# A two-block network on one core: the second experts' ring begun in the output projection, step sizes made with heads on partitions, eight slots for the first experts, and matmuls that fill waits

## The chip, the cores and the metric

The kernel runs on one core of one Trainium2 chip. The metric is the device time of the whole program in microseconds (us), the median of several runs; lower is better. TensorE is called PE, VectorE DVE, ScalarE ACT, GpSimd POOL and SyncE SP, as in the profile.

## The reference

The input x is 512 tokens of width 1024, and all data is float32. Two blocks follow one another.

The first block projects the tokens (and 256 context tokens) into neighbourhood attention and a bidirectional state-space scan with 32 heads in each direction. For the scan, each token has a step size per head and direction, `dt = softplus(dt_raw + bias)`, where `dt_raw` is 64 columns of the input projection; with `a = -dt * exp(a_log)` the scan needs sums of `a` over the tokens of each piece of 128 (four pieces of x, two of the context): up to each token, after it, and over the whole piece. The 24 tiles of the scan's inputs pass a convolution over five tokens. Branches, gates and an output projection close the mixer. Then come 16 experts, each of which takes the 64 tokens that rate it highest:

```python
gate, idx = lax.top_k(jnp.transpose(aff, (0, 2, 1)), cap)
hid = silu(xg @ w_eg) * (xg @ w_eu)
yo = (hid @ w_ed) * gate
```

The second block has an RWKV mixer, latent attention and an output projection `w_out`, and then 32 smaller experts, of which each token uses two; a last rmsnorm with a gain gives the output.

## The kernel before, in words

The program is a row of stages. Each stage is a block in which every engine runs its own list in order and waits on semaphores; the next block begins when all engines have left the last one. Float32 matmuls appear in the trace as two PE instructions each, transposes as one. Weights come over SP's DMA queue, mostly in pieces of 2 MB (`PIECE`, 16 KB on each of 128 partitions).

**The convolution stage**, `steps_and_conv`. PE first makes the step-size products: for each of six pieces of tokens and each of eight blocks of the contraction it loads 128 tokens as weights and streams 64 columns of `w_dt` (L1119), 48 matmuls in all. DVE adds the bias; then come an exponential and a logarithm on ACT and a chain of small DVE operations (L1240 to L1252) which ends in `a`. Meanwhile PE begins the 24 tiles (L1141): 8 matmuls of 512 columns each, and from the fifth tile on also 8 of 256 columns for the context (L1147). Each tile needs one of two banks, and a bank comes free when DVE has convolved its tile (`main_taken`). DVE's order is: bias and signs, tile 0, the chain, tile 1, tile 2 and so on. After tile 3, PE makes the sums: 36 matmuls of 32 columns (L1130), whose exponentials ACT makes. From tile 5 on PE turns the finished tiles back.

**The first experts.** `route_tokens` norms the rows, scores them, and turns the affinities so that experts lie on partitions (L2255, waits for `aff_ready`). DVE then finds the 64 best of each (L2288 to L2294) in eight rounds of two operations, PE waits for `chosen_T`, turns the marks back (L2259) and counts them (L2265). `stream_experts` gathers tokens with matmuls (L2040) and streams 192 weight pieces through a ring of `EC_SLOTS` = 7 slots. The first 7 are loaded in `route_tokens`; SP loads piece n once PE is done with piece n - 7. The eight pieces of the first pair's gate weights are the first eight.

**The end of the second mixer.** `project_rows_onto` multiplies by `w_out` in two halves of 512 columns (stage `p_out2`), each loaded in the stages before. Its input `u2T` was freed after it.

**The second experts.** `RoundsRing` has nine slots of one piece. `route_experts` loads the router's weights and the constants, then pieces 0 to 2, then waits for the normed rows, stores them to memory (`hm_xn_rows`), and loads pieces 3 to 8. `fine_experts` builds the token lists of each pair of experts (L3657), gathers the rows by an indirect DMA from POOL (L3637), turns them (`flips`, L3665), and multiplies (`hidden`, L3677, and `down`, L3696). POOL also issues for each first piece an indirect DMA which would load other experts in a second round and moves nothing in the first (`load_again`, L1905); `hidden` waits for it too. SP reloads a slot when its product is done, 39 pieces in all.

**The last norm**, `final_norm`. ACT squares and sums four tiles of rows, then takes one root of all four; DVE takes the reciprocal and scales the four tiles, each of which SP stores.

Of the kernel before, what the change touches and what calls it, by code (L numbers as in the profile page):

```python
# [15 lines left out]
P = 128  # L16
D = 1024
# [262 lines left out]
def rows_view(x):  # L280

    return x[0].rearrange("(t p) d -> p t d", p=P)

# [789 lines left out]
def steps_and_conv(k, hT, hcT, steps_in, weights, vec, taps, work, dt, a, dec, bcT, b_rows, bc_rows, xs, xsc):  # L1073
# [9 lines left out]
    with ctx:  # L1083
        main, side = ps("main", [P, 2, 512]), ps("side", [P, 2, 512])
        flip, flip_c = ps("flip", [P, 2, 512]), ps("flip_c", [P, 2, 512])
        prod, sums = flip[:, 0, :], (flip[:, 1, :], flip_c[:, 0, :], flip_c[:, 1, :])
# [86 lines left out]
        def _(act):  # L1173
# [14 lines left out]

            act.wait_ge(steps_loaded, 16 * 5)
# [6 lines left out]
            for i in range(3):  # L1196
                act.activation(dec[:, 4 * i:4 * i + 4, :].rearrange("p m n -> p (m n)"), sums[i][:, 0:384], ACT.Exp).then_inc(exp_out, 1)
# [413 lines left out]
def project_rows_onto(k, label, w, kt, xT, residual, n_chunks, ahead):  # L1611
# [13 lines left out]
    project(k, label, w, kt, 512, n_chunks, groups, add, ahead=ahead, first=wait_loaded)  # L1625
# [190 lines left out]
EC_SLOTS = 7  # L1816
# [43 lines left out]
HM_SLOTS = 9  # L1860

# [9 lines left out]
class RoundsRing:  # L1871
# [3 lines left out]
    def __init__(self, k, scope):  # L1875
# [8 lines left out]
        self.tile = scope.enter_context(k.nc.sbuf_tensor("hm_ring", [P, HM_SLOTS, PIECE], F32))  # L1884
        self.rows = scope.enter_context(k.nc.sbuf_tensor("hm_again_rows", [P, 2 * LT], mybir.dt.uint32))
        self.first_loaded = [k.semaphore(f"hm_first_loaded{n}") for n in range(HM_SLOTS)]
        scope.callback(lambda: k.clear(self.first_loaded))

    def load_first(self, sp, slots):
        for n in slots:  # L1890
            sp.dma_start(*second_weights(self.k, self.tile[:, n, :], *self.order[n])).then_inc(self.first_loaded[n], 16)
# [4 lines left out]
    def load_again(self, pool, n):  # L1896
        kind, u, e = self.order[n]
        pool.wait_ge(self.first_loaded[n], 16)
        if kind == "gu":
            parts = [(self.tile[:, n, :], self.k.dram["moe_w_gu_2"][0].rearrange("e (p a) n -> (e p) (a n)", p=P), 2 * u + e)]  # L1900
        else:
            parts = [(self.tile[:, n, i * PIECE // 2:(i + 1) * PIECE // 2], self.k.dram["moe_w_down_2"][0].rearrange("e (p f) n -> (e p) (f n)", p=P), 2 * u + i)
# [9 lines left out]
    def load(self, sp, n):  # L1912
        sp.dma_start(*second_weights(self.k, self.tile[:, n % HM_SLOTS, :], *self.order[n])).then_inc(self.loaded[n % HM_SLOTS], 16)

    def wait(self, pe, *job):
# [6 lines left out]
        return self.tile[:, n % HM_SLOTS, :]  # L1922
# [273 lines left out]
def route_tokens(k, norm, out, router, columns, ring, rank, aff):  # L2196
# [8 lines left out]
    with ctx:  # L2205
# [35 lines left out]
        def _(pe):  # L2241
# [1089 lines left out]
def second_mixer(k, x_in, dump=None):  # L3331
# [16 lines left out]
    with ExitStack() as outer:  # L3348
        uT = tile(outer, "u2T", [P, KD, L])
        with ExitStack() as mid:  # L3350
# [552 lines left out]
```

## Time and profile before

| | |
|---|---|
| median of 3 runs | 3594.27 us (3591.18 to 3597.16) |
| the profiled execution | 3598.31 us, of which the span 3596.5 us |
| busy: PE, weight loads, DVE, ACT, POOL | 3148.0, 1667.6, 1070.2, 558.9, 286.4 us |
| moved by DMA | 669.33 MB, mean 186 GB/s |
| mean granted clock of PE | 0.931 of full speed |

The span runs from the first to the last instruction of the profiled execution. Matmuls are pipelined, so a group's time includes a modelled end. The granted clock of PE is 1.00 (2.4 GHz) or 0.50 (1.2 GHz); a number between says that a stretch has both. GB/s and the DMA share (1.00: all 16 engines busy) show where the weights set the pace.

### The profile page before, as it was taken

To read this page: it belongs to the slowest core of one execution; us is meant where nothing else is said; L and a number is where in the kernel's file an instruction comes from. 1 tells how busy PE (TensorE), PEld (TensorE's weight loads), DVE (VectorE), ACT (ScalarE), POOL (GpSimd) and SP (SyncE) were. 2 spreads that over 40 slices of the span, in tenths; PEclk is the share of its full clock that TensorE was granted. 3 is DMA by queue.
4 is the path that set the end of the run, shared out by engine and by line. 5 is a ranking of instruction groups with operands and counts; after the bars stand their busy time and mean duration, and the time that the engine had idled before them with its cause. 6 is when DMAs were issued, how large, how long until landed. Compare 5 with 4: busy or idle time off the path is not lost. (4 is left out here: it accounts for less than half of the span.)

```text
span 3596.5 us, 37828 instructions
## 1 busy us (share of the span) xinstructions
PE 3148.0 (88%) x15792; PEld 1667.6 (46%) x15792; DVE 1070.2 (30%) x2063; ACT 558.9 (16%) x1178; POOL 286.4 (8%) x270
## 2 busy tenths in 40 slices
PE   6997889998899999698999999987996789995984
PEld 5444645664554444453344434433545763643331
DVE  2233702454573301410111011103056553522112
ACT  2002510112452200100000000002022221301111
POOL 0003000002761000000000000000002200001000
PEclk9998998998899999699999999998998999996997
DMA  7721021110001222379999999996310021017996
GB/s 264 257 71 47 2 74 35 47 36 0 24 1 47 94 70 70 164 295 428 424 425 428 424 424 412 421 423 277 128 35 2 3 109 49 12 59 275 404 425 259
DMA packets 132079, 669.33 MB, mean 186 GB/s; under 512 B 17578, under 2 KB 45645, under 8 KB 98889
## 3 DMA queue, kind: packets, MB, share of 16 engines
q1 hardware_dynamic: 115385, 630.24, 43.5%
q10 hardware_dynamic: 11488, 28.31, 2.1%
q0 software_dynamic: 5040, 8.40, 0.7%
q8 instruction: 124, 2.03, 0.2%
q14 instruction: 42, 0.34, 0.0%
HBM read 672.15 MB, written 14.69 MB: 191 GB/s over the span
## 5 line engine op out<-in xcount | busy, mean ns | idle before, releaser
L1992 PE MATMUL ec_wide<-ec_ring,ec_xg 128*64 128x512 f32 x2048 | 456.7, 600 | 20.8 <-issue 15.4
L1992 PEld LDWEIGHTS ec_wide<-ec_ring,ec_xg 128*64 128x64 f32 x2048 | 148.1, 138 | 309.3 <-issue 305.1
L2026 PE MATMUL ec_acc<-ec_ring,ec_hidT 128*64 128x512 f32 x1024 | 238.8, 622 | 36.4 <-DMA ec_ring<-in_w_exp_down 34.5
L2151 DVE TENSOR_SCALAR ec_xg<-ec_piece,ordered 128x128 f32<-128x128 f32 x64 | 21.9, 405 | 579.7 <-PE ec_piece L2040 579.7
L2026 PEld LDWEIGHTS ec_acc<-ec_ring,ec_hidT 128*64 128x64 f32 x1024 | 84.9, 143 | 188.1 <-issue 188.1
L3677 PE MATMUL hm_gu<-hm_ring,hm_xg 128*64 128x512 f32 x512 | 121.3, 629 | 15.8 <-DMA hm_ring<-in_moe_w_gu,hm_again_rows 7.7
L2040 PEld LDWEIGHTS ec_piece<-ec_sel,x 128*128 128x128 f32 x512 | 122.9, 336 | 8.6 <-issue 5.7
L2040 PE MATMUL ec_piece<-ec_sel,x 128*128 128x128 f32 x512 | 124.4, 406 | 2.8 <-DVE ec_sel L2133 2.8
L2727 POOL TENSOR_TENSOR solve_T<-const_rw,solve_T 128x512 f32<-128x512 f32 x8 | 10.1, 1266 | 1321.3 <-DVE solve_T L2765 1321.3
L2115 ACT ACTIVATE ec_hidT<-ec_acc 128x512 f32<-128x512 f32 x32 | 17.4, 594 | 516.1 <-PE ec_acc L2015 516.1
L1141 PE MATMUL conv_main<-hT,conv_early 128*128 128x512 f32 x192 | 86.2, 605 | 1.6 <-DVE bcT L1217 1.6
L561 PE MATMUL p_rkv_acc<-ahead_rkv,h2mT 128*128 128x384 f32 x256 | 85.9, 500 | 1.9 <-DVEq L569 1.9
L1141 PE MATMUL conv_main<-hT,conv_late 128*128 128x512 f32 x192 | 86.8, 607 | 0.0
L3677 PEld LDWEIGHTS hm_gu<-hm_ring,hm_xg 128*64 128x64 f32 x512 | 39.8, 145 | 94.4 <-issue 92.7
L1389 ACT ACTIVATE ssd_seg_in<-const_all,a 128x128 f32<-128x128 f32 x256 | 77.8, 389 | 0.5 <-PEq L1083 0.5
L2166 DVE TENSOR_TENSOR branch<-branch,ec_piece 128x512 f32<-128x512 f32 x64 | 44.0, 688 | 108.8 <-PE ec_piece L2058 108.8
L1349 PE MATMUL ssd_seg<-ssd_seg_in,const_all 128*128 128x512 f32 x128 | 62.8, 614 | 10.0 <-DVE ssd_cbm L1411 10.0
L2058 PE MATMUL ec_piece<-ec_y,ec_selT 128*128 128x512 f32 x128 | 63.8, 623 | 7.3 <-DVE ec_selT L2160 6.1
L561 PEld LDWEIGHTS p_rkv_acc<-ahead_rkv,h2mT 128*128 128x128 f32 x256 | 50.2, 196 | 37.4 <-issue 2.7
L3696 PE MATMUL hm_acc<-hm_ring,hm_hidT 128*64 128x512 f32 x256 | 64.3, 649 | 2.1 <-ACT hm_hidT L3728 1.6
L2772 DVE TENSOR_TENSOR solve_T<-solve_T,solve_wide 64x512 f32<-64x512 f32 (+1 forms) x80 | 50.6, 632 | 50.0 <-PE solve_wide L2658 42.0
L1375 PE MATMUL ssd_yd<-ssd_xd,ssd_lx 128*128 128x64 f32 x512 | 61.6, 274 | 2.1 <-DVE ssd_lx L1415 2.1
(624 smaller groups left out, 4957.3 us busy)
## 6 DMA issues: line engine op xcount, KB each, us to landing
ec_ring<-in_w_exp_gate SPq DMA_DIRECT2D x64, 2048.0 KB, 13.6
ec_ring<-in_w_exp_up SPq DMA_DIRECT2D x64, 2048.0 KB, 22.2
ec_ring<-in_w_exp_down SPq DMA_DIRECT2D x64, 2048.0 KB, 17.3
hm_ring<-in_moe_w_gu SPq DMA_DIRECT2D x32, 2048.0 KB, 27.3
hm_ring<-in_moe_w_down SPq DMA_DIRECT2D x16, 2048.0 KB, 29.1
ahead_qkv<-in_w_in SPq DMA_DIRECT2D x10, 2048.0 KB, 9.6
key<-in_w_ada ACTq DMA_DIRECT2D x4, 2048.0 KB, 8.7
v<-in_w_ada ACTq DMA_DIRECT2D x4, 2048.0 KB, 10.2
```

What stands on the lines that cost most here:

```text
L561: last = pe.matmul(acc[0:rows, bank, 0:cols], stat(j), mov(j), start=(j == 0), stop=(j == kt - 1))
L1141: last = pe.matmul(main[:, i % 2, :], w[:, j, m * P:(m + 1) * P], hT[:, j, :], start=(j == 0), stop=(j == KD - 1))
L1349: pe.matmul(seg[:, h, :], k.const("after" if d == 0 else "before"), seg_in[:, m % 2, 4 * h:4 * h + 4].rearrange("p h l -> p (h l)"), start ...
L1375: last = pe.matmul(yd[:, m % 2, h * 64:(h + 1) * 64], lx[:, m % 2, h, :], xd[:, n % 2, h * 64:(h + 1) * 64], start=True, stop=True)
L1389: ins = act.activation(seg_in[:, m % 2, h, :], cum, ACT.Copy, scale=a[:, tile(units[mains[m]]), col:col + 1])
L1992: last = pe.matmul(wide[half(e), b, :], xg[:, u % 2, j, half(e)], w[e][:, a, b * 512:(b + 1) * 512], start=(j == 0), stop=(j == KD - 1))
L2026: last = pe.matmul(acc[half(e), h, :], hidT[:, f, half(e)], w[e][:, r, h * 512:(h + 1) * 512], start=(f == 0), stop=(f == FT - 1))
L2040: last = pe.matmul(piece[:, m % 2, i * P:(i + 1) * P], x[:, t, HALF * h + i::KD], sel[:, t, :], start=(t == 0), stop=(t == LT - 1))
L2058: pe.matmul(piece[:, m % 2, :], selT[:, t * P:(t + 1) * P], y[:, h * 512:(h + 1) * 512], start=True, stop=True).then_inc(piece_done, 1)
L2772: dve.tensor_tensor(x, x, wide[s][half(c), c, first * 256:512], ALU.subtract).then_inc(T_done[s], 1)
L3677: last = pe.matmul(gu[half(e), u % 2, :], xg[:, u % 2, j, half(e)], w[e][:, j, :], start=(j == 0), stop=(j == KD - 1))
L3696: last = pe.matmul(acc[half(e), h, :], hidT[:, u % 2, f * P + e * SLOTS:f * P + (e + 1) * SLOTS], view[:, e * FT + f, h * 512:(h + 1) * 51 ...
```

## The change

1. `steps_and_conv`: the products are made with `w_dt` as weights (64 columns, so that heads lie on partitions) and the tokens streaming, 8 matmuls of 512 columns and 8 of 256. ACT copies them to SBUF, and after tile 0 PE turns them with six transposes (`step_rows`). The sums are 6 matmuls of 192 columns in place of 36 of 32.
2. `EC_SLOTS` is 8.
3. `keep_clocked` issues matmuls whose result nobody reads: 12 before the wait for `aff_ready`, 72 before that for `chosen_T`, and 12 in `fine_experts` ahead of the first turn.
4. `u2T` stays allocated through the second experts and becomes the last of the nine slots. Seven slots are placed before `p_out2`, and their loads are issued there by SP (`also`); the last two are loaded in `route_experts`. SP's six loads behind the store of the rows are gone.
5. `final_norm` loads the root's table first, and takes root, reciprocal and scaling tile by tile.

The rest of the diff is indentation in `second_mixer`.

```diff
+def keep_clocked(k, pe, bank, n):
+    for _ in range(n):
+        pe.matmul(bank[:, 0:P], k.const("ones"), k.const("ident"), start=True, stop=True)
...
-        prod, sums = flip[:, 0, :], (flip[:, 1, :], flip_c[:, 0, :], flip_c[:, 1, :])
+        prod, sums = flip[:, 1, :], (flip[:, 0, :], flip_c[:, 0, :], flip_c[:, 1, :])
+        stepsT = work[0:64, 3, 2 * n:2 * n + L + CTX]
...
                 pe.wait_ge(steps_loaded, 16 * 5)
+                for bank, src, width in ((flip, hT, L), (flip_c, hcT, CTX)):
+                    for j in range(KD):
+                        last = pe.matmul(bank[0:64, 0, 0:width], w_dt[:, j, :], src[:, j, :], start=(j == 0), stop=(j == KD - 1))
+                    last.then_inc(products_T, 1)
+
+            def step_rows():
+                pe.wait_ge(steps_taken, 2)
                 for t in range(N_SEG):
-                    src, c = (hT, t) if t < LT else (hcT, t - LT)
-                    for j in range(KD):
-                        last = pe.matmul(prod[:, t * 64:(t + 1) * 64], src[:, j, c * P:(c + 1) * P], w_dt[:, j, :],
-                                         start=(j == 0), stop=(j == KD - 1))
+                    last = pe.transpose(prod[:, t * 64:(t + 1) * 64], stepsT[:, t * P:(t + 1) * P], k.const("ident", 64)[:, 0:64])
                 last.then_inc(product_ready, 1)
...
-                for d in range(2):
-                    for t in range(N_SEG):
-                        m = d * N_SEG + t
-                        for i, name in enumerate((("upto", "after", "ones"), ("from", "before", "ones"))[d]):
-                            c = (m % 4) * 96 + i * 32
-                            last = pe.matmul(sums[m // 4][:, c:c + 32], k.const(name), a[:, t, d * 32:(d + 1) * 32], start=True, stop=True)
+                for i, names in enumerate((("upto", "from"), ("after", "before"), ("ones", "ones"))):
+                    for d, name in enumerate(names):
+                        last = pe.matmul(sums[i][:, d * N_SEG * 32:(d + 1) * N_SEG * 32].rearrange("p (t h) -> p t h", h=32), k.const(name),
+                                         a[:, :, d * 32:(d + 1) * 32], start=True, stop=True)
...
                 project_tile(i)
+                if i == 0:
+                    step_rows()
...
+            act.wait_ge(products_T, 1)
+            act.activation(stepsT[:, 0:L], flip[0:64, 0, :], ACT.Copy).then_inc(steps_taken, 1)
+            act.wait_ge(products_T, 2)
+            act.activation(stepsT[:, L:L + CTX], flip_c[0:64, 0, 0:CTX], ACT.Copy).then_inc(steps_taken, 1)
...
-EC_SLOTS = 7
+EC_SLOTS = 8
...
             norm.turn(pe, scores)
+            keep_clocked(k, pe, norm.pt[:, 0, :], 12)
             pe.wait_ge(aff_ready, 1)
...
             last.then_inc(wide_ready, 1)
+            keep_clocked(k, pe, norm.pt[:, 0, :], 72)
             pe.wait_ge(chosen_T, 1)
...
-            project_rows_onto(k, "p_out2", k.dram["w_out_2"][0], KD, uT, k.residual, 2, ahead)
+    k.rounds_ring = RoundsRing(k, k.second_scope, uT[:, :, :].rearrange("p j n -> p (j n)"))
+    project_rows_onto(k, "p_out2", k.dram["w_out_2"][0], KD, uT, k.residual, 2, ahead,
+                      also=lambda sp: k.rounds_ring.load_first(sp, range(HM_HEAD)))
...
-            ring.load_first(sp, range(3))
+            ring.load_first(sp, range(HM_HEAD, HM_SLOTS))
             sp.wait_ge(norm.row_ready, LT)
             sp.dma_start(xn_rows.rearrange("(t p) d -> p t d", p=P), norm.xn[:, :, :]).then_inc(xn_stored, 16)
-            ring.load_first(sp, range(3, HM_SLOTS))
...
             lists(1)
+            pe.wait_ge(index_ready, 2)
+            keep_clocked(k, pe, list_, 12)
             flips(0)
...
+            act.preload_act_table(ACT.Sqrt)
             for t in range(LT):
                 link(act.activation(square[:, :], x[:, t, :], ACT.Square, accum_out=ss[:, t:t + 1]))
-            act.activation(rstd[:, :], ss[:, :], ACT.Sqrt, scale=1.0 / D, bias=k.const("eps")).then_inc(root_ready, 1)
+                act.activation(rstd[:, t:t + 1], ss[:, t:t + 1], ACT.Sqrt, scale=1.0 / D, bias=k.const("eps")).then_inc(root_ready, 1)
...
-            link(dve.reciprocal(rstd[:, :], rstd[:, :]))
             for t in range(LT):
+                dve.wait_ge(root_ready, t + 1)
+                link(dve.reciprocal(rstd[:, t:t + 1], rstd[:, t:t + 1]))
```

## Rows read from the trace of the kernel before

**Rows 1.** Stretches (us from the start): busy time and count of each engine, PE clock, DMA share, GB/s

```profile
582.00:603.00 21.00, 20.55 (x97) 20.58 (x98) 0.09 (x1) 1.54 (x2) 0.00 (x0) 0.52 0.32 100
```

**Rows 2.** Timeline of PE in the convolution stage: start, length, instruction, count, wait before

```profile
582.45 13.59 PE L1119 MATMUL conv_flip<-w_dt,hT 128*128 128x64 f32 x64 [2.60 <-PEq L1058]
...
602.66 22.82 PE L1141 MATMUL conv_main<-hT,conv_early 128*128 128x512 f32 x48
627.12 7.13 PE L1141 MATMUL conv_main<-hT,conv_early 128*128 128x512 f32 x16 [1.64 <-DVE bcT L1217]
634.09 2.76 PE L1130 MATMUL conv_flip<-a,const_all 128*128 128x32 f32 x24
636.68 9.80 PE L1130 MATMUL conv_flip_c<-a,const_all 128*128 128x32 f32 x48
646.30 9.46 PE L1141 MATMUL conv_main<-hT,conv_late 128*128 128x512 f32 x16
655.60 3.62 PE L1147 MATMUL conv_side<-hcT,conv_late 128*128 128x256 f32 x16
```

**Rows 3.** Timeline of DVE in the same stage: tile 0, the chain's first operation, tile 1

```profile
611.78 0.75 DVE L1213 TENSOR_SCALAR bcT<-conv_main,taps 128x512 f32<-128x512 f32 x1 [7.33 <-PE conv_main L1141]
...
615.59 0.35 DVE L1240 TENSOR_SCALAR y<-y 128x384 f32<-128x384 f32 x1
...
623.18 0.74 DVE L1213 TENSOR_SCALAR bcT<-conv_main,taps 128x512 f32<-128x512 f32 x1
```

**Rows 4.** Timeline of PE in the first routing and at the first gather

```profile
1506.05 1.02 PE L2255 MATMUL route_wide<-const_all,ec_aff 128*16 128x128 f32 x4 [1.59 <-DVE ec_aff L2286]
1520.49 0.61 PE L2259 MATMUL route_score<-const_all,route_chosenT 16*128 16x16 f32 x4 [13.42 <-DVE route_chosenT L2294]
1521.42 4.45 PE L2265 MATMUL route_spread<-route_chosen,const_all 128*128 128x16 f32 x20 [0.32 <-DVE route_chosen L2296]
1528.65 15.55 PE L2040 MATMUL ec_piece<-ec_sel,x 128*128 128x128 f32 x64 [2.79 <-DVE ec_sel L2133]
```

**Rows 5.** A stretch in that gather: columns as in rows 1

```profile
1534.50:1536.00 1.50, 1.50 (x9) 1.50 (x7) 0.00 (x0) 0.00 (x0) 0.00 (x0) 0.80 0.00 0
```

**Rows 6.** Stretches of the first experts: all of the stream, and a slow one

```profile
1556.00:2474.00 918.00, 856.45 (x3720) 370.90 (x3716) 110.81 (x264) 43.63 (x71) 0.00 (x0) 0.98 1.00 423
2200.00:2250.00 50.00, 50.00 (x220) 17.42 (x222) 10.04 (x20) 2.17 (x4) 0.00 (x0) 1.00 0.99 409
```

**Rows 7.** Waits of PE in the first experts: us in total, times, longest

```profile
PE ec_acc L2026 <- DMA ec_ring<-in_w_exp_down: 34.5, 18, 2.7
```

**Rows 8.** A stretch that holds most of the output projection

```profile
3198.00:3246.00 48.00, 48.00 (x113) 21.32 (x112) 4.82 (x7) 0.00 (x0) 0.00 (x0) 1.00 0.00 0
```

**Rows 9.** Timeline at the start of the second experts: gather, empty load, turn, product

```profile
3289.04 1.20 POOL L3637 DMA_INDIRECT hm_xrow<-hm_xn_rows,hm_index  x1 [0.91 <-POOL hm_xrow L3631]
...
3293.54 0.99 POOL L1905 DMA_INDIRECT hm_ring<-in_moe_w_gu,hm_again_rows  x1 [0.31 <-issue]
...
3298.85 1.97 PE L3665 MATMUL hm_flip<-const_all,hm_xrow 128*128 128x128 f32 x8 [8.90 <-DMA hm_xrow<-hm_xn_rows,hm_index]
...
3308.56 9.49 PE L3677 MATMUL hm_gu<-hm_ring,hm_xg 128*64 128x512 f32 x32 [7.74 <-DMA hm_ring<-in_moe_w_gu,hm_again_rows]
```

**Rows 10.** The eleven empty loads of L1905, from issue to landing

```profile
DMA to landing us min/median/max: 4.7/10.0/14.9
```

**Rows 11.** Timeline of PE: one later pair's first product

```profile
3353.81 7.04 PE L3677 MATMUL hm_gu<-hm_ring,hm_xg 128*64 128x512 f32 x32
```

**Rows 12.** A stretch of the second experts' stream: columns as in rows 1

```profile
3350.00:3540.00 190.00, 170.42 (x814) 71.10 (x814) 30.11 (x58) 22.49 (x37) 11.86 (x12) 0.94 1.01 425
```

**Rows 13.** Timeline of the last norm, ACT and DVE

```profile
3580.61 1.06 ACT L3813 ACTIVATE final_square<-x 128x1024 f32<-128x1024 f32 x1 [23.03 <-PEq L3854]
...
3585.32 1.28 ACT L3814 ACT_TABLE_LOAD   x1
...
3587.16 4.87 DVE L3823 SCALAR_TENSOR_TENSOR final_y<-x,final_rstd,final_gain 128x1024 f32<-128x1024 f32 x4
```

More of the change, by code:

```diff
@@ L1196, in _ @@
             for i in range(3):
-                act.activation(dec[:, 4 * i:4 * i + 4, :].rearrange("p m n -> p (m n)"), sums[i][:, 0:384], ACT.Exp).then_inc(exp_out, 1)
+                act.activation(dec[:, :, 32 * i:32 * i + 32], sums[i][:, 0:2 * N_SEG * 32].rearrange("p (m h) -> p m h", h=32), ACT.Exp).then_inc(exp_out, 1)
             act.wait_ge(exp_out, 6)
@@ L1608, in branch, with project_rows_onto @@
     project(k, label + "_b", w, feats, width, D // width, groups, merge, link_steps=1 if add else 0, ahead=ahead, then=then)
-def project_rows_onto(k, label, w, kt, xT, residual, n_chunks, ahead):
+def project_rows_onto(k, label, w, kt, xT, residual, n_chunks, ahead, also=None):
     x = residual.tile
@@ L1623, in wait_loaded @@
         dve.wait_ge(residual.loaded, 16)
-    project(k, label, w, kt, 512, n_chunks, groups, add, ahead=ahead, first=wait_loaded)
+    project(k, label, w, kt, 512, n_chunks, groups, add, ahead=ahead, first=wait_loaded, also=also)
 def project_rows(k, label, w, kt, xT, out, n_chunks, width=512, ahead=None, then=None, also=None):
@@ L1860 @@
 HM_SLOTS = 9
+HM_HEAD = HM_SLOTS - 2
 def second_weights(k, place, kind, u, e):
@@ L1871, with __init__ @@
 class RoundsRing:
-    def __init__(self, k, scope):
+    def __init__(self, k, scope, last):
         self.k = k
@@ L1883, in __init__, with complete @@
         self.index = {job: n for n, job in enumerate(self.order)}
-        self.tile = scope.enter_context(k.nc.sbuf_tensor("hm_ring", [P, HM_SLOTS, PIECE], F32))
-        self.rows = scope.enter_context(k.nc.sbuf_tensor("hm_again_rows", [P, 2 * LT], mybir.dt.uint32))
+        self.head = scope.enter_context(k.nc.sbuf_tensor("hm_ring", [P, HM_HEAD, PIECE], F32))
+        self.places = [self.head[:, n, :] for n in range(HM_HEAD)] + [None, last]
         self.first_loaded = [k.semaphore(f"hm_first_loaded{n}") for n in range(HM_SLOTS)]
         scope.callback(lambda: k.clear(self.first_loaded))
+    def complete(self, scope):
+        self.places[HM_HEAD] = scope.enter_context(self.k.nc.sbuf_tensor("hm_ring_late", [P, PIECE], F32))[:, :]
+        self.rows = scope.enter_context(self.k.nc.sbuf_tensor("hm_again_rows", [P, 2 * LT], mybir.dt.uint32))
     def load_first(self, sp, slots):
         for n in slots:
-            sp.dma_start(*second_weights(self.k, self.tile[:, n, :], *self.order[n])).then_inc(self.first_loaded[n], 16)
+            sp.dma_start(*second_weights(self.k, self.places[n], *self.order[n])).then_inc(self.first_loaded[n], 16)
     def enter(self, sem):
@@ L1912, in load @@
     def load(self, sp, n):
-        sp.dma_start(*second_weights(self.k, self.tile[:, n % HM_SLOTS, :], *self.order[n])).then_inc(self.loaded[n % HM_SLOTS], 16)
+        sp.dma_start(*second_weights(self.k, self.places[n % HM_SLOTS], *self.order[n])).then_inc(self.loaded[n % HM_SLOTS], 16)
     def wait(self, pe, *job):
@@ L1921, in wait @@
             pe.wait_ge(self.loaded[n % HM_SLOTS], 16 * (n // HM_SLOTS))
-        return self.tile[:, n % HM_SLOTS, :]
+        return self.places[n % HM_SLOTS]
 def stream_experts(k, ring, x, rstd, rank, gate, scale_cols, shift_cols, out):
@@ L3606, in fine_experts @@
         BACK = 2 * LT
-        back = ring.tile[:, 0:BACK * D // PIECE, :].rearrange("p s (b n) -> p (s b) n", n=D)
+        back = ring.head[:, 0:BACK * D // PIECE, :].rearrange("p s (b n) -> p (s b) n", n=D)
         gu, turn, acc, flip, list_ = ps("gu", [P, 2, 512]), ps("turn", [P, 512]), ps("acc", [P, 2, 512]), ps("flip", [P, 2, 512]), ps("list", [P, 512])
@@ L3836, in second_experts @@
         out = k.residual.tile
-        with ExitStack() as s:
-            ring = RoundsRing(k, s)
+        with k.second_scope as s:
+            ring = k.rounds_ring
+            ring.complete(s)
             ordered = tile(s, "hm_ordered", [P, KD])
@@ L3873, in two_blocks @@
         k.ordered = tile(everything, "ordered", [P, 2, KD])
-        k.branch_scope = ExitStack()
+        k.branch_scope, k.second_scope = ExitStack(), ExitStack()
         first_mixer(k, dram["x"])
```

187 lines of the change are left out of this document (93 added, 94 removed).

## The prediction, made before the changed kernel was run

> **What bounds the kernel now.** No single resource does: each stage has its own. I read first the stretches of the whole span, then in each stage that the change touches the timeline of PE, then that of the engine or queue that PE waits for.
>
> In the convolution stage PE is the bound. From 582.45 to 655.60, from the step products to the end of tile 4's 512-column matmuls, it stands still only for the 1.64 us ahead of tile 3 [rows 2]. But its clock is at 0.52 while it makes the step products [rows 1], which are 96 small instructions, and the 48 later sums (9.80 us) take 0.204 us each where the first 24 (2.76 us) took 0.115 [rows 2]: both clock levels in one list. The tiles that follow pay too: 9.46 us where a tile takes 7.03 to 7.13 [rows 2].
>
> In the first experts DMA is the bound: from 1556 to 2474 all 16 engines are busy (share 1.00, 423 GB/s), and PE waits for weights 18 times, 34.5 us in all [rows 6, 7]. The stream begins when PE gives back the first slot, soon after the first gather [rows 4].
>
> At the start of the second experts the ring's own first filling is in the way. The gather issued at 3289.04 is turned at 3298.85 and `hidden(0)` begins at 3308.56, after waits of 8.90 and 7.74 us for DMA [rows 9]; no product waits there. After that DMA is again the bound (share 1.01, 425 GB/s) [rows 12], so what the first product gains, the end gains. The last norm is a plain chain [rows 13].
>
> **Step products and sums.** Old, to the end of tile 4's main matmuls: 655.60 - 582.45 = 73.15 us [rows 2]. New: 16 instructions of 512 columns at the 7.03 us of a tile and 16 of 256 at 3.62 us [rows 2], about 10.5 without the modelled ends. The old products ran at half clock, and the three tiles behind them lost 22.82 - 3 x 6.9 = 2.1 us till the clock was back; I charge the same 2.1 at the entry (0 if the clock holds). Tile 0: 6.9. Then DVE leads. In the old kernel tile 3 starts 627.12 - 611.7 = 15.4 us after tile 0 is ready: its convolution (611.78 to 615.59), the chain (to 623.18), tile 1 (to 627.1) [rows 2, 3]. In the new one the bias and signs no longer hide behind tile 0, because they follow `step_rows`. Six transposes and their latency are about 0.9 us (four turns take 0.61 or 1.02 at half clock [rows 4]), three DVE operations of 384 columns, between 0.35 and 0.75 each [rows 3], about 1.5. So tile 3 starts 17.8 us after tile 0, and PE waits some 3.4 us ahead of it. Tile 3: 6.9. Sums: 12 instructions of 192 columns at 6.9/16 x 192/512 = 0.16 us, 1.9 with 0.2 of latency. Tile 4: 6.9. I add 1 us for a clock that may fall in the 3.4 us wait. Sum: 10.5 + 2.1 + 6.9 + 17.8 + 6.9 + 2.1 + 6.9 + 1.0 = 54.2. **Saved: 19 us**, between 15 (the clock falls at both places and the tiles after wait too) and 22 (it never falls). ACT's two copies hide behind tile 0; if they didn't, only `step_rows` would move. The exponentials of the sums are the same three and stand ahead of tile 5's end. The convolution weights are asked for by PE's progress with an idle queue (share 0.32 even in the busiest part [rows 1]).
>
> **Eighth slot.** A piece takes 918/185 = 4.96 us of the stream [rows 6]. Eight pieces lie ready instead of seven, 184 are left, the start is the same event. PE can follow: its 34.5 us of waits [rows 7] is slack that it uses up first. **Saved: 5 us**; 3 if part of the waits isn't given back, 5 at most. The eighth load has room before the stream begins: the queues are empty during the gather (share 0.00) [rows 5].
>
> **The 84 filling matmuls of the first routing.** PE works in order, so what they overrun delays the chain to the first gather, and with it the whole stream. A call is two instructions with 128 weight columns. The nearest rows are the sums: 0.115 us at full clock, 0.204 at half [rows 2], so 0.22 or 0.41 a call (a shade less without the latency). The 12 take 2.6 to 4.9 us in a wait of 1.59 us; the 72 take 15.5 to 29.4 us in a wait of 13.42 us [rows 4]. The clock is at half when they start; the gather, also of 128 columns, brought it back some 6 us after its start [rows 4, 5]. I take that: the 12 at half clock, 3.3 us late, and nearly all 72 at full, 2.6 us more than their wait, so PE turns the marks back about 6 us later than now. Given back: 4.45 us of counts become 2.3, and 0.61 becomes 0.4, so 2.4 us. The gather itself gains nothing: its 64 instructions take 0.243 us each on both sides of the change of clock [rows 4, 5]. **Lost: 3.5 us**, between 0 (full clock at once) and 9 (it comes late).
>
> **The ring begun in the output projection.** Seven pieces are 35 us of DMA. In 3198 to 3246 the queues carry nothing (share 0.00) [rows 8], so they are down by about 3230, ahead of the router's small loads. SP has nothing else to issue there; `w_out`'s second half is ahead of them in the same queue. The last two pieces and the store of the rows are 15 us of DMA early in the routing, and the store has two pieces ahead of it, not three, and none behind. So at 3289 DMA is idle. The gather should land in about 4.7 us, the shortest that the empty loads took [rows 10], at 3293.8. The 12 filling calls wait for the second list, about 1.1 us after the gather's issue (an estimate: POOL issues the second gather and the first empty load before 3293.54 [rows 9]), and run from 3290.2 to 3295.1 at half clock; the turn takes 1.97 [rows 9] and DVE's scaling of 1024 elements 1.2 to 1.3 (4.87/4 [rows 13]), together 3298.4. The second empty load, issued at 3293.54, lands at 3298.2 [rows 9, 10]. `hidden(0)` starts at about 3298.4 instead of 3308.56. **Saved: 10 us**, 7 if the empty load is slow by itself (its median is 10.0 [rows 10]), 11 if an idle queue is faster than any row. The stream behind it is DMA-bound [rows 12] and moves with it.
>
> Its first product takes 9.49 us where later ones take 7.04 [rows 9, 11], and the clock shapes the second too; the 12 calls may bring it back before. Between 0 and 5 us; I take **2 us**. Here a row and a rule differ in what they promise: what lies between the calls and the product is eight transposes and DVE's scaling.
>
> **Last norm.** Old: 3580.61 to 3592.03, 11.4 us [rows 13]. New: table 1.28, first squares and root 1.5, then four times DVE's 0.2 + 1.25, 8.8 us. The gain's load starts with the stage and may hold the first row; **saved 2 us**, between 1 and 3.
>
> **Sum.** 19 + 5 - 3.5 + 10 + 2 + 2 = 34.5 us. The profiled execution took 3598.3, so 3563.8 on its scale; it stands 4.0 us above the median of the runs. On the median: 3594.3 - 34.5 = 3559.8.
>
> **Rivals.** (a) *The clock stays at half through the filling matmuls of the routing.* For it: the 20 instructions of the counts, back to back, still ran at half clock (4.45 us) [rows 4]. Against: the gather of the same width brought it back [rows 5]. Then 72 calls take 29.4 us, PE is 3.3 + 16 us late and the counts gain nothing: 19.3 lost in place of 3.5, 3575.6. Chance 0.09.
> (b) *The clock is half again at `hidden(0)`.* The turn in the old kernel takes 1.97 us, half clock's time [rows 9]. Then the 2 us go: 3561.8. Chance 0.22. The Trainium skill's page "TensorE: Matmul & The Clock Gate" ("Part 4: PE-mode transpose") says that transposes don't count as busy for the clock; by that rule the eight turns give up what the twelve calls won, and the time is this rival's. No row of ours has such a burst followed by turns alone.
> (c) *PE, not DMA, paces the first experts once the slot is there,* and the eighth gives 0: 3564.8. PE was busy 856 of 918 us [rows 6]. Against it stand 18 waits up to the end [rows 7]. Chance 0.06.
> (d) *The ring's seven loads hold up `w_out`'s second half.* If all eight transfers shared the queue, it would land 40 us after the stage's start, and PE wants it in the middle of a stage of some 55 us, of which 48 are in [rows 8]: about 11 us late, 3570.8. Chance 0.04.
> (e) *Slower than before:* one more transfer in flight lowers the rate of the first experts' stream. The stretch at 2200 had 409 GB/s with the engines no less busy [rows 6]. 184 pieces take 913 us at 423 GB/s; each 1% of rate is 9 us, and from 3.8% (407 GB/s, all through) the kernel is slower than before; at 5% about 3606. Against: the queue is full already and its depth alone would be new. Chance 0.02.
> (f) *The reordered start of the convolution costs more than its 2.4 us,* say tile 1's convolution held by ACT's tables: half the 19 us gone, 3569. Chance 0.06.
>
> **Chances and range.** My forecast has the remaining 0.51. From the terms' bounds it alone reaches from 3551 to 3569; (b) and (c) lie inside. Taking in (d), (f) and most of (a), and some luck with the clock below, the range is 3548 to 3574. About 0.2% (7 us) is what a measurement here tells from no change. Only (e), or several bounds together, reach 3587: faster 0.96, within 0.2% 0.01, slower 0.03.
>
> **What would show it.** Right: tile 3's first matmul 36 to 39 us after the products' first (44.7 now [rows 2]), with a wait of 3 to 4 us ahead; twelve sums in about 2 us; a stream of 184 pieces at 423 GB/s; L2259 some 5 to 7 us later after the scores than now; no DMA between 3230 and the router's loads (on the old scale); `hidden(0)` 9 to 11 us sooner after the gather's issue; 9 us of last norm. Wrong: the 72 calls in over 20 us; a wait of PE for `w_out`; a new DMA wait for the empty loads; a stream rate under 415 GB/s.

## The result, and the profile after

The changed kernel takes 3548.98 us (median of 4 runs, 3546.7 to 3553.64) where the kernel before, on the same chip, takes 3593.66 (3591.18 to 3597.16): a ratio of 0.9877, 95% interval 0.986 to 0.9894, 44.7 us saved. On two more chips the ratio was 0.9871 and 0.9876. The prediction was 34.5 us saved, 3559.8 us; the result lies at the low end of its range (3548 to 3574), and below the 3551 to 3569 that the forecast's own terms reached. The profiled executions have spans of 3596.5 and 3548.5 us, so 48.0 us are to be found between them. The same events in both, in us from the start:

| event | before | after | difference | since the row above |
|---|---|---|---|---|
| first step product | 582.45 | 582.60 | +0.15 | |
| behind tile 4's wide matmuls | 655.60 | 636.69 | -18.91 | -19.06 |
| first routing: first turn of PE | 1480.48 | 1459.76 | -20.72 | -1.81 |
| first gather on PE | 1528.65 | 1510.74 | -17.91 | +2.81 |
| last weights of the first experts used | 2484.3 | 2453.3 | -31.0 | -13.1 |
| second experts: first gather issued | 3289.04 | 3259.00 | -30.04 | +1.0 |
| `hidden(0)` begins | 3308.56 | 3267.76 | -40.80 | -10.76 |
| its weights given back (SP reloads) | 3318.08 | 3274.89 | -43.19 | -2.39 |
| last product read out | 3556.56 | 3510.52 | -46.04 | -2.85 |
| last norm begins | 3580.61 | 3535.50 | -45.11 | +0.93 |
| its last multiplication ends | 3592.03 | 3544.64 | -47.39 | -2.28 |

The timeline of PE in the convolution stage of the changed kernel (start, length, instruction, count, the wait before it and what ended it), to be read beside [rows 2]:

```profile
582.60 8.75 PE L1126 MATMUL conv_flip<-hT,w_dt 128*64 128x512 f32 x16 [2.60 <-PEq L1064]
591.18 3.62 PE L1126 MATMUL conv_flip_c<-hcT,w_dt 128*64 128x256 f32 x16
594.73 7.13 PE L1151 MATMUL conv_main<-hT,conv_early 128*128 128x512 f32 x16
601.79 0.58 PE L1132 MATMUL conv_flip<-const_all,y 64*128 64x64 f32 x6
602.31 14.00 PE L1151 MATMUL conv_main<-hT,conv_early 128*128 128x512 f32 x32
619.21 8.83 PE L1151 MATMUL conv_main<-hT,conv_early 128*128 128x512 f32 x16 [2.90 <-DVE bcT L1233]
627.88 0.81 PE L1139 MATMUL conv_flip<-a,const_all 128*128 128x192 f32 x4
628.53 1.46 PE L1139 MATMUL conv_flip_c<-a,const_all 128*128 128x192 f32 x8
629.83 7.03 PE L1151 MATMUL conv_main<-hT,conv_late 128*128 128x512 f32 x16
```

The 96 narrow products have become 12 us. The sums, 72 instructions in 12.2 us before, are now 12 in 1.95 us. Both falls of the clock are to be seen: 8.75 us where a tile takes 7.03 to 7.13, and 8.83 behind the wait of 2.90 us.

The same view in the first routing and at the first gather, beside [rows 4]:

```profile
1483.57 4.79 PE L288 MATMUL route_pt<-const_all 128*128 128x128 f32 x24
...
1488.64 16.24 PE L288 MATMUL route_pt<-const_all 128*128 128x128 f32 x144
...
1505.55 2.40 PE L2288 MATMUL route_spread<-route_chosen,const_all 128*128 128x16 f32 x20 [0.32 <-DVE route_chosen L2319]
1510.74 15.55 PE L2061 MATMUL ec_piece<-ec_sel,x 128*128 128x128 f32 x64 [2.79 <-DVE ec_sel L2154]
```

Twelve calls at half clock in 4.79 us, 72 at full clock in 16.24, no wait behind either; the counts take 2.40 in place of 4.45, and the gather the same 15.55 as before.

Stretches of the whole stream of the first experts (length, busy time of the engines, then the clock of PE, the DMA share and GB/s), and PE's waits in it, beside [rows 6, 7]:

```profile
1538.00:2445.00 907.00, 854.14 (x3718) 368.12 (x3716) 110.69 (x264) 43.63 (x71) 0.00 (x0) 0.98 1.00 426
```

```profile
PE ec_acc L2047 <- DMA ec_ring<-in_w_exp_down: 28.4, 14, 2.7
```

The rate is 426 GB/s where it was 423. Less than 1%, but of 900 us.

The timeline at the start of the second experts, beside [rows 9]:

```profile
3259.00 1.20 POOL L3660 DMA_INDIRECT hm_xrow<-hm_xn_rows,hm_index  x1 [0.90 <-POOL hm_xrow L3654]
...
3259.69 5.49 PE L288 MATMUL hm_list<-const_all 128*128 128x128 f32 x24 [0.25 <-DVE hm_index L3775]
...
3264.97 1.48 PE L3688 MATMUL hm_flip<-const_all,hm_xrow 128*128 128x128 f32 x8
...
3266.48 1.22 DVE L3781 TENSOR_TENSOR hm_xg<-hm_flip,hm_ordered 128x1024 f32<-128x1024 f32 x1 [6.17 <-PE hm_flip L3688]
...
3267.76 7.09 PE L3700 MATMUL hm_gu<-hm_ring,hm_xg 128*64 128x512 f32 x32 [1.32 <-DVE hm_xg L3781]
```

Neither the turn nor the product waits for DMA any longer; the DMA share in 3258 to 3275 is 0.16. The eleven empty loads now land in (beside [rows 10]):

```profile
DMA to landing us min/median/max: 2.1/2.9/9.7
```

And the last norm, beside [rows 13]:

```profile
3535.52 0.34 SPq L3828 DMA_DIRECT2D final_gain<-in_final_norm_g  x1
3536.79 1.06 ACT L3839 ACTIVATE final_square<-x 128x1024 f32<-128x1024 f32 x1
...
3537.97 0.29 ACT L3840 ACTIVATE final_rstd<-final_ss,const_all 128x1 f32<-128x1 f32 x1
...
3538.98 0.16 DVE L3848 RECIPROCAL final_rstd<-final_rstd 128x1 f32<-128x1 f32 x1 [5.89 <-DMA final_gain<-in_final_norm_g]
...
3543.36 1.28 DVE L3849 SCALAR_TENSOR_TENSOR final_y<-x,final_rstd,final_gain 128x1024 f32<-128x1024 f32 x1
```

The gain's load, 3.44 us from issue to landing on the chain that ended last, is what DVE waits for; the first root is ready at 3538.26, 0.7 us sooner.

So most terms came out as forecast, and one did not: between the first gather and the last weights of the first experts the changed kernel gained 13.1 us where one piece of 4.96 us was charged.

### The profile page after: what moved, and what is told of

It reads as the page before. It is cut to its first block and busy times, and to the rows that moved or that the text cites. A ratio compares the mean times of both kernels' runs of the same rounds, so it can differ in the third digit from the quotient of the medians.

```text
span 3548.5 us, 38000 instructions
## 1 busy us (share of the span) xinstructions
PE 3138.4 (88%) x15866; PEld 1657.4 (47%) x15866; DVE 1070.3 (30%) x2066; ACT 560.3 (16%) x1183; POOL 287.7 (8%) x270
## 5 line engine op out<-in xcount | busy, mean ns | idle before, releaser
L2047 PE MATMUL ec_acc<-ec_ring,ec_hidT 128*64 128x512 f32 x1024 | 233.6, 611 | 29.2 <-DMA ec_ring<-in_w_exp_down 28.4
L1391 PEld LDWEIGHTS ssd_yd<-ssd_xd,ssd_lx 128*128 128x128 f32 x512 | 61.2, 196 | 2.9 <-DVE ssd_lx L1431 2.9
## 6 DMA issues: line engine op xcount, KB each, us to landing
ec_ring<-in_w_exp_gate SPq DMA_DIRECT2D x64, 2048.0 KB, 17.7
```

The lines of the kernel that those rows point to most:

```text
L1391: last = pe.matmul(yd[:, m % 2, h * 64:(h + 1) * 64], lx[:, m % 2, h, :], xd[:, n % 2, h * 64:(h + 1) * 64], start=True, stop=True)
L2047: last = pe.matmul(acc[half(e), h, :], hidT[:, f, half(e)], w[e][:, r, h * 512:(h + 1) * 512], start=(f == 0), stop=(f == FT - 1))
```

## Experiments

### The eighth slot

```
EC_SLOTS = 8   again: unchanged
EC_SLOTS = 7   slots7
EC_SLOTS = 6   slots6
EC_SLOTS = 8   before8, in the kernel before (there it was 7)
```

Expected of the changed kernel run once more:

> The changed kernel once more. The stream of the first experts ran at 426 GB/s in its first profile (1538 to 2445) and at 423 in the kernel before (1556 to 2474). Theory A (the rate belongs to the eighth slot): 426 to 428 GB/s again, and 43 to 48 us saved. Theory B (the rate is drawn anew in each execution): it may come out at 420 to 424 this time, and then the span is 6 to 9 us longer than 3548.5. The clock's phase alone may move the span by 2 to 3 us.

Expected with seven slots:

> The changed kernel with seven slots in the first experts' ring; nothing else. Forecast (one reload fewer, one piece of 4.96 us): 5 us slower than the changed kernel, stream at the same rate. Theory A (eight transfers under way also keep the rate up): 12 to 14 us slower, stream at 422 to 424 GB/s with stretches under 420. Theory B (rate drawn anew): 5 us by the medians, whatever the rate in the profile. Rival C (PE paces the stream): no difference.

Expected of the kernel before with eight:

> The kernel before with eight slots in the first experts' ring; nothing else. Forecast: 5 us faster than the kernel before, all of it between the first gather and the last weights. Theory A: 12 to 14 us faster, stream at 426 to 428 GB/s. Theory B: 5 us by the medians. Rival C: no difference.

Expected with six, after these three were known:

> The changed kernel with six slots in the first experts' ring; nothing else. Eight slots went to seven at a price of 17 us. Theory A (with fewer slots the queue runs dry at the places of each pair of experts where PE gives nothing back for up to 21.7 us): the dry spells grow faster than the slots shrink, 30 to 70 us slower than with seven, with 10 us stretches under 300 GB/s. Rival D (a full queue moves more bytes a second than a less full one, everywhere): some 17 us again, and a rate that is lower in all stretches. Forecast of the prediction (one reload for each slot): 5 us.

The column "stream" is from the first product of the first experts to the last use of their weights in the profile. "Missing" sums what the rate lacks of 428 GB/s, as time, over stretches of 10 us from 12 to 14 us after the stream's start to near its end (what is above 428 is taken off).

| kernel | slots | median, us | ratio to the kernel before | stream, us | missing, us |
|---|---|---|---|---|---|
| before | 7 | 3596.59 | 1 | 938.6 | 10.2 |
| before8 | 8 | 3580.05 | 0.995 (0.9936 to 0.9964) | 925.5 | 2.1 |
| again | 8 | 3551.73 | 0.9871 (0.9856 to 0.9886) | 926.0 | 3.1 |
| slots7 | 7 | 3569.01 | 0.9919 (0.9905 to 0.9932) | 950.7 | 22.0 |
| slots6 | 6 | 3598.28 | 1.0012 (1.0002 to 1.0021) | 977.4 | 44.3 |

The first four medians are of one chip: the slot is worth 16.5 us in the kernel before and 17.3 us in the changed one. That is nearest to theory A, and more than its 12 to 14 us. Theory B falls: the eleven profiles with eight slots (those of the runs below among them) have streams of 923.8 to 928.5 us, and the two with seven 938.6 and 950.7. The two with seven slots are one profile each of two kernels, and that of slots7 was the slowest of its five executions (3573.26 us); why they differ by 12 us wasn't tried. So the 13.1 us between the first two profiles are one draw, and the medians' 17 the better figure. Rival C falls too. slots6 ran on another chip, beside a fourth run of the changed kernel (again2, below): 48.2 us slower than that, so the second slot is worth some 31 us, the low end of what theory A gave (30 to 70). The two columns on the right say how a longer stream divides, not why: with seven slots the stream is 24.7 us longer than in again, of which one reload is 4.96 and the missing time 22.0 - 3.1 = 18.9; with six it is 51.4 longer, two reloads and 41.2 us.

Where the time is missing is seen in stretches of 10 us. First the kernel with six slots, then the one with seven, then the changed kernel, each around 1700:

```profile
1690.00:1700.00 10.00, 10.00 (x44) 10.00 (x43) 1.37 (x4) 0.00 (x0) 0.00 (x0) 1.00 0.99 421
1700.00:1710.00 10.00, 10.00 (x46) 6.06 (x47) 3.24 (x12) 0.00 (x0) 0.00 (x0) 1.00 0.71 301
1710.00:1720.00 10.00, 9.13 (x42) 3.07 (x40) 1.38 (x2) 0.00 (x0) 0.00 (x0) 1.00 0.79 316
...
1750.00:1760.00 10.00, 10.00 (x52) 3.83 (x52) 0.00 (x0) 1.09 (x2) 0.00 (x0) 1.00 1.02 436
```

```profile
1690.00:1700.00 10.00, 10.00 (x45) 7.38 (x46) 3.27 (x13) 0.00 (x0) 0.00 (x0) 1.00 1.02 431
1700.00:1710.00 10.00, 9.13 (x42) 3.07 (x40) 1.38 (x2) 0.00 (x0) 0.00 (x0) 1.00 0.96 393
1710.00:1720.00 10.00, 10.00 (x36) 3.20 (x34) 3.44 (x5) 0.00 (x0) 0.00 (x0) 1.00 0.94 356
```

```profile
1700.00:1710.00 10.00, 9.12 (x40) 3.11 (x39) 1.38 (x2) 0.00 (x0) 0.00 (x0) 1.00 1.00 428
1710.00:1720.00 10.00, 10.00 (x38) 3.21 (x38) 4.50 (x7) 0.00 (x0) 0.00 (x0) 1.00 1.00 428
```

The engines of DMA are idle for up to three tenths of these stretches (share 0.71), while PE is busy for over nine tenths of them; outside these places the rate with six slots is as high as with eight (436; 26 of its 95 stretches are at 430 or more, and 28 of the 90 of again), so rival D, which wanted it lower everywhere, falls. The place comes back every 120 us, once for each pair of experts. What happens there shows in the timelines of PE and of SP's issues with six slots:

```profile
1688.63 15.55 PE L2061 MATMUL ec_piece<-ec_sel,x 128*128 128x128 f32 x64
1704.12 7.09 PE L2013 MATMUL ec_wide<-ec_ring,ec_xg 128*64 128x512 f32 x32
```

```profile
1668.95 20.59 SPq L1852 DMA_DIRECT2D ec_ring<-in_w_exp_up  x6
1711.24 10.38 SPq L1852 DMA_DIRECT2D ec_ring<-in_w_exp_gate  x4
```

PE makes the gather of the next pair, 15.5 us of small matmuls that use no weights of the ring, and then a product of 7.1 us before it gives any back. SP issues nothing from 1689.5 to 1711.2: its longest wait is 21.7 us in the kernels with six, seven and eight slots alike. The ring must hold enough that is asked for and not yet landed to carry the queue over this.

How much that is can be counted from the traces: the pieces that SP has issued, less the bytes of its queue that have landed. In the six later pairs some 4.5 pieces land between the two issues. The wait begins with 3.6 to 4.2 pieces on their way with six slots, with 4.3 to 5.2 with seven (in slots7 and in the kernel before) and with 5.4 to 6.2 with eight. It ends with none, with 0 to 0.6 and with 0.9 to 1.7. So six slots run dry, seven all but dry, and eight keep about a piece or more.

The kernel before had the same holes, flatter. Its gather ends at 2190.3 and SP's next issue is at 2197.5; the rate is lowest after that:

```profile
2208.00:2218.00 10.00, 10.00 (x39) 3.18 (x39) 4.82 (x7) 0.00 (x0) 0.00 (x0) 1.00 0.96 385
2218.00:2228.00 10.00, 10.00 (x44) 3.15 (x39) 4.54 (x12) 0.00 (x0) 0.00 (x0) 1.00 0.96 377
```

The same two stretches have 429 GB/s in before8. Idle engines are only part of what is missing: 377 is 0.88 of 428, and the share is 0.96. Summed over all stretches, the lower share makes up about 34 of the 41.2 us with six slots, and about 10 of the 18.9 with seven. The rest passed with the engines counted as busy, behind the places where few pieces were on their way. Why they move less then wasn't tried; rival D may hold there, though not everywhere.

### The filling calls of the first routing

```
-            keep_clocked(k, pe, norm.pt[:, 0, :], 12)     no84: gone    trim, best: 4
-            keep_clocked(k, pe, norm.pt[:, 0, :], 72)     no84: gone    trim: 50    best: 58
```

> The changed kernel without the 84 filling calls of the first routing (12 and 72); they compute nothing that is used. My step: the calls overrun the waits by some 5 us and give back 2.3 us in marks and counts, so without them the time from the end of the scores to the first gather is 2.8 us shorter (27.1 in the changed kernel, about 24.3 here) and the kernel 3 us faster; marks take 0.61 and counts 4.45 us again. Rival (the calls' clock reaches the gather and the first pieces): the gather takes longer than 15.55 us or the first pieces run at half clock for longer, and the kernel is 0 to 5 us slower than the changed one.

> The changed kernel with 4 and 50 filling calls in the first routing in place of 12 and 72; they compute nothing that is used. If the calls only cost what they overrun the waits by, and keep the clock: the marks are turned back some 15.5 to 16.5 us after the end of the scores (21.2 in the changed kernel, 16.0 without calls in the kernel before), in 0.4 us, the counts take 2.4, and the kernel is 4.5 to 5.5 us faster than the changed one and 2 us faster than the one without calls. Rival (the clock comes back too late in fewer calls): the counts take 4.45, and 50 calls run past their wait; 0 to 3 us faster.

Measured: without calls 3549.63 us, 2.1 less than the changed kernel on the same chip (ratio 0.987, 0.9855 to 0.9885), which the times alone can't tell from nothing. The trace can: from the first turn to the first gather it is 48.1 us (1458.7 to 1506.84), where the changed kernel takes 50.9 to 51.0 and the kernel before 48.2. The calls cost 2.8 us, as stepped; the gather is no slower for their absence, so the rival falls.

With 4 and 50 calls: 3544.15 us, ratio 0.985 (0.9834 to 0.9867), 4 to 6 us less than the changed kernel by the times, as expected. But that agreement is luck: from turn to gather it takes 47.9 us, 3.1 less than the changed kernel and no better than without calls. The step failed, for a reason that the timeline of PE shows:

```profile
1485.73 11.82 PE L288 MATMUL route_pt<-const_all 128*128 128x128 f32 x100
1499.36 0.42 PE L2282 MATMUL route_score<-const_all,route_chosenT 16*128 16x16 f32 x4 [1.81 <-DVE route_chosenT L2317]
1500.09 4.18 PE L2288 MATMUL route_spread<-route_chosen,const_all 128*128 128x16 f32 x20 [0.32 <-DVE route_chosen L2319]
```

The marks, right behind a wait of only 1.81 us, still took 0.42 us, as at full clock. The granted clock is 1.00 until 1500.4 and 0.50 after that, so the counts ran at half clock for most of their 4.18 us. Fifty calls are too few, 72 too many; hence 58 in the next kernel, which also has this ahead of tile 3 of the convolution stage:

```
             for i in range(N_TILES):
+                if i == R - 1:
+                    keep_clocked(k, pe, sums[0], 12)
                 project_tile(i)
```

> The changed kernel with 4 and 58 filling calls in the first routing in place of 12 and 72, and with twelve filling calls added ahead of tile 3 of the convolution stage, where PE waits 2.90 us for tile 1's convolution (into the bank that the sums take later); no filling call computes anything that is used. With 50 calls the clock fell in the 1.81 us that were left of the wait, and the counts took 4.18 us; 58 should fill it. Expected: counts in 2.4 us, first gather 1.8 us sooner after the scores than with 4 and 50 calls (4.9 sooner than in the changed kernel); tile 3 in 7.0 us in place of 8.83. In all 5 to 7 us faster than the changed kernel. Rival (the clock falls at another place instead, since it is drawn): 2 to 4 us.

Its timeline of PE in the routing:

```profile
1485.29 14.01 PE L288 MATMUL route_pt<-const_all 128*128 128x128 f32 x116
1499.24 0.42 PE L2284 MATMUL route_score<-const_all,route_chosenT 16*128 16x16 f32 x4
1499.97 2.40 PE L2290 MATMUL route_spread<-route_chosen,const_all 128*128 128x16 f32 x20 [0.32 <-DVE route_chosen L2321]
```

The 58 calls end as the marks arrive, the counts take 2.40, and from turn to gather it is 46.4 us (1458.8 to 1505.17), 4.6 less than in the changed kernel. The median is 3544.52 us, 5.5 under the changed kernel's 3550.07 on the same chip (ratios 0.9853, 0.9836 to 0.9869, and 0.9876, 0.9859 to 0.9892: they overlap a little), within the 5 to 7 expected. Not all that the trace shows as gained at the gather arrives: the stream then takes 928.5 us in place of 926, so 2.5 us of the gain are gone at its end. Why this stream is longer wasn't tried.

The change in the convolution stage alone:

> The changed kernel with twelve filling calls ahead of tile 3 of the convolution stage alone; they compute nothing that is used. Where the clock fell in that wait, tile 3 took 8.83 us; in one execution it didn't fall and the tile took 7.13. Expected: the calls end within the wait of 2.90 us, tile 3 takes 7.0 to 7.13 us, and 1.7 us are saved against the changed kernel, under what the times can tell. Rival (the calls run past the wait): 0 or slower.

```profile
616.08 2.84 PE L288 MATMUL conv_flip<-const_all 128*128 128x128 f32 x24
619.14 7.13 PE L1151 MATMUL conv_main<-hT,conv_early 128*128 128x512 f32 x16 [0.22 <-DVE bcT L1235]
```

Tile 3 takes 7.13 us in place of 8.83; tile 4 begins 45.5 us after the first product in place of 47.2. The median is 3549.91 (0.9875, 0.9858 to 0.9891): 1.7 us are under what the times can tell, as expected.

The changed kernel beside these two and slots6:

> The changed kernel, as a measure for the three others of this chip: 0.987 of the kernel before, 3547 to 3552 us.

It took 3550.07 us, 0.9876; its stream 926.1 us.

### The start of the second experts

```
 ringlate
-                      also=lambda sp: k.rounds_ring.load_first(sp, range(HM_HEAD)))
-            ring.load_first(sp, range(HM_HEAD, HM_SLOTS))
+            ring.load_first(sp, range(3))                  ahead of the store of the rows
+            ring.load_first(sp, range(3, HM_SLOTS))        behind it
 no12
-            keep_clocked(k, pe, list_, 12)
```

> The changed kernel with the first nine pieces of the second experts' ring asked for where they were before: three ahead of the stored rows in the second routing, six behind them. My step (10 us): 9 to 12 us slower than the changed kernel; the first product of the second experts starts some 19 us after the first gather's issue in place of 8.8, after waits for DMA. Rival (the ring's filling would be hidden by the twelve filling calls or by the routing itself): under 4 us.

> The changed kernel without the twelve filling calls ahead of the first turn of the second experts; they compute nothing that is used. My step (2 us, the clock): the turn takes 1.9 to 2.0 us and the first product 9.4 in place of 1.48 and 7.09, and the first weights are given back 2 to 3 us later after the gather's issue. Rival (b), the Trainium skill's rule on transposes in the page on TensorE and the clock gate: it speaks of what the turns count for, and the changed kernel's trace has already gone against it here (7.09 us); by it this run would be the same as the changed kernel.

ringlate took 3561.98 us, ratio 0.9909 (0.9893 to 0.9926), 12 us more than the changed kernel (0.0034 of 3595). The changed kernel did not run on this chip; its ratio is taken as 0.9875, near its three (0.9871, 0.9876, 0.9877). The timeline of POOL, then of PE, has the same 19 us from the gather's issue to the product as before the change:

```profile
3256.70 1.20 POOL L3660 DMA_INDIRECT hm_xrow<-hm_xn_rows,hm_index  x1 [0.90 <-POOL hm_xrow L3654]
```

```profile
3266.20 1.53 PE L3688 MATMUL hm_flip<-const_all,hm_xrow 128*128 128x128 f32 x8 [3.33 <-DMA hm_xrow<-hm_xn_rows,hm_index]
...
3275.26 9.65 PE L3700 MATMUL hm_gu<-hm_ring,hm_xg 128*64 128x512 f32 x32 [7.53 <-DMA hm_ring<-in_moe_w_gu,hm_again_rows]
```

The twelve filling calls were in this kernel too, and the turn has full clock (1.53); but behind the 7.53 us of waiting the product takes 9.65, in place of 7.09. The DMA share in 3258 to 3275 is 0.85 in this kernel, in the changed one 0.16. The early ring saves the wait, 9.8 us (18.56 in place of 8.76), and keeps what the calls win; with the 2.6 us of the product that is the 12 of the medians.

no12 took 3552.36 us (0.9878, 0.9862 to 0.9895), about 1 us more, too little for the times. In its trace:

```profile
3257.41 1.20 POOL L3660 DMA_INDIRECT hm_xrow<-hm_xn_rows,hm_index  x1 [0.90 <-POOL hm_xrow L3654]
```

```profile
3261.97 1.94 PE L3688 MATMUL hm_flip<-const_all,hm_xrow 128*128 128x128 f32 x8 [4.13 <-DMA hm_xrow<-hm_xn_rows,hm_index]
...
3265.23 9.86 PE L3700 MATMUL hm_gu<-hm_ring,hm_xg 128*64 128x512 f32 x32 [1.32 <-DVE hm_xg L3780]
```

The product starts 7.82 us after the gather's issue (8.76 with the calls) and ends at 17.7 (15.85 with them). Without calls the turn starts 4.56 us after the issue, when the gather has landed, and with them 5.97; at the product 0.9 us of that is left, and the product itself is 2.8 shorter: 1.8 us won, against 2 in the sum.

### The step products undone

```
 convold: steps_and_conv as in the kernel before, the rest as changed
```

> The changed kernel with the step products, rows and sums of the kernel before (96 and 48 narrow products); nothing else. My step (19 us, 18.9 read between the traces): 19 us slower than the changed kernel by the trace, at the first wide products of the tile behind the sums; 17 to 21 by the medians. Rival (the later stages absorb part of it, since the stream of the first experts starts from the routing and its ring was asked for earlier): under 15.

3567.41 us, ratio 0.992 (0.9903 to 0.9936): 16 us more than the changed kernel (0.0045 of 3595), a little less than expected. By the trace the tile behind the sums ends at 655.63, so the whole 18.9 us are there. Against again it is 20.9 at the first product of the first experts and 20.3 at their last weights. At the second routing's first turn only 17.0 are left (3238.1 against 3221.1). The branch product ahead of the second mixer's output projection came out 1.4 us shorter in this run (29.1 in place of 30.5), and the projection itself 1.7: its last instruction starts 54.5 us after its first, in again 56.2, and its longest took 0.67 us, there 1.06 (half clock). The rival falls: the stream absorbed nothing. In the trace the missing us went further on, at places where the clock differed by chance; the medians alone don't tell 16 from 17 to 21.

## Why the prediction was right, and where it was not

The range was met by luck. The prediction let its own terms reach from 3551 to 3569; all their best bounds added are 46 us, that is 3548.3, and all their worst 17 us, 3577. The result, 3548.98, is in the range only where every term is near its best or by the room for "some luck with the clock". Neither is what happened: most terms came out near their forecast, and one, the slot, gave 12 us more than its best bound of 5.

**Step products and sums: right.** Forecast 19, found 19.06 between the profiles and 16 by the medians of convold. The two costs of the clock that were charged with 2.1 and 1 were 1.7 and 1.8; the wait ahead of tile 3 was 2.90 for 3.4; tile 3 starts 36.6 us after the first product, in the 36 to 39 that were given.

**Eighth slot: the step that failed.** "Saved: 5 us; 3 if part of the waits isn't given back, 5 at most." The term charged the reload alone and was worth 16.5 to 17.3 by the medians (13.1 between the two profiles). The premise was that "DMA is the bound: all 16 engines are busy (share 1.00)", and that PE's 34.5 us of waits were the only slack. But PE and DMA took turns in waiting. A share of 1.00 over 918 us, and 0.99 with 409 GB/s over the slow 50 [rows 6], hid stretches of 0.96 and 377 GB/s. That slow stretch was in hand, and was read as evidence for rival (e), that one more transfer in flight lowers the rate; it followed on the queue running down to 0.2 pieces, and with one more in flight (before8) it is gone. Rival (e) has the sign of the effect wrong. Rival (c), PE as the pace, is answered by both: before8 is 16.5 us faster, and PE has 28.4 us of waits left.

**The 84 calls: right.** 3.5 forecast, 2.8 found, with the split as stepped: 12 at half clock (4.79 us for a wait of 1.59), 72 at full, overrunning together by 5.2 us; counts 2.40 and marks 0.42 give 2.2 back. Rival (a) did not come.

**The ring in the output projection: right.** 10 forecast, 10.76 between the profiles, 9.8 in ringlate. The gather, put at 4.7 us, lands in about 4.6 in no12, where nothing else holds the turn. In the changed kernel the twelve calls hold the turn until 5.97 us after the gather's issue, near the 6.1 of the forecast (3289.04 to 3295.1), and the gather has landed by then: the turn waits for nothing. Rival (d) did not come: `w_out`'s second half was not late.

**The clock at `hidden(0)`: right.** 2 forecast, 2.39 between the profiles, 1.8 against no12. Rival (b) fell. The Trainium skill ("TensorE: Matmul & The Clock Gate", "Part 4: PE-mode transpose") has it that transposes don't count as busy for the clock; the eight turns (1.48 us) and 1.32 us of waiting did not give up full clock here: the product took 7.09, in this profile and in nine others with the same calls and no wait for DMA. Whether turns count isn't settled by this; it shows only that full clock outlasted them and the wait.

**Last norm: right.** 2 forecast, 2.28 found; the gain's load does hold the first row, by 0.7 us. This is read from the two profiles; no run has the norm alone.

**Not in the sum:** 1.8 us between the convolution stage and the routing, the 2.85 us of the second experts' stream, less 1.0 and 0.93 that were lost elsewhere. convold shows how such amounts arise, with a projection that is 1.7 us shorter in one run than in another of the same code; for the 2.85 nothing was tried. The slot's term is what separates the forecast from the median: 34.5 + 12 = 46.5, where three comparisons gave 44.7 to 46.5. What the runs gave for each part agrees: 16.2 (convold), 17.3 (slots7), 12.2 (ringlate, with the product behind it), -2.1 (no84) and the norm's 2.3 are 45.9.

## What to carry to other kernels

A ring of prefetched weights must cover the longest time in which its consumer gives nothing back, not the mean: what counts is how many pieces are still on their way when that time begins. Before pricing a slot, take that time from the queue's own waits (here 21.7 us in every pair) and look at the DMA share in stretches shorter than it: a mean of 1.00 over hundreds of microseconds can hide a nearly dry queue, and then a slot is worth several times its one transfer (5 us by the count, 17 measured, 31 for the one before it). Matmuls that only fill a wait should end with it: a few too many delay the chain, and with a few too few the clock can fall behind what is left of the wait, and the fillers have bought nothing.

## What the runs showed that was not expected

- The worth of slots grows fast as they get fewer: 6 to 7 some 31 us, 7 to 8 17 us, for 4.96 us of transfer each.
- The clock can fall behind a wait as short as 1.81 us that follows 11.82 us of unbroken work (counts 4.18 us instead of 2.40), and it falls after the work has begun again: 0.3 us into the counts there, 1.3 us into tile 3 in the changed kernel (granted clock 1.00 until 620.5, then 0.52 and 0.50). It doesn't do so always: behind the same wait of 2.9 us tile 3 took 8.83 us in seven profiles and 7.13 in two, no84 and ringlate, with the same code up to there.
- An indirect load that moves nothing lands in 2.1 us at the least and 2.9 in the median of the eleven, six of them issued with a DMA share of 0.16; behind the ring's first loads the median was 10.0 [rows 10].
- With the table of the square root asked for first and the four tiles of rows done one by one, DVE and not ACT sets the pace of the last norm: its multiplications start 1.39 us apart and are 1.28 long.
